# First norm by feature, gate columns behind the modulation stages, and split square sums in a hybrid recurrent layer

## The reference

```python
def rmsnorm(x, w):
    xf = x.astype(jnp.float32)
    y = xf * lax.rsqrt(jnp.mean(jnp.square(xf), axis=-1, keepdims=True) + EPS)
    return (y * w.astype(jnp.float32)).astype(x.dtype)
...
        mod = jax.nn.silu(c) @ w_ada[l] + b_ada[l]
        sh1, sc1, g1, sh2, sc2, g2 = [m[:, None, :] for m in jnp.split(mod, N_MOD, axis=-1)]
        h = rmsnorm(x, norm_mix[l]) * (1.0 + sc1) + sh1
...
    proj = h @ w_in
    hq, hf, hi, hog, gq, gk, gv, ga, gb, gz, gate_a, gate_b = split_cols(proj, IN_SIZES)
...
    o_hg = rmsnorm(o_hg, hg_norm) * jax.nn.silu(heads(hog, HG_DV).astype(jnp.float32))
...
    conv_out, s_conv_new = causal_conv(jnp.concatenate([gq, gk, gv], axis=-1), s_conv, conv_w)
```

## Time and profile before

| | |
|---|---|
| median of 3 runs | 949.81 us (949.46 to 950.88) |
| the profiled execution, its own time | 951.82 us |
| its span in the profile | 950.0 us |
| busy: PE | 923.8 us (97%) |
| busy: DVE | 669.4 us (70%) |
| busy: ACT | 438.2 us (46%) |
| busy: POOL | 105.6 us (11%) |

### The profile page before, as it was taken

The page is one execution under the profiler, slowest core; times in us unless marked ns, Lnnn a source line. Parts: engine busy times, 40 slices in busy tenths (PEclk is TensorE's granted clock), DMA queues, the critical chain, the costliest instruction groups (busy, mean ns, idle before and its releaser), DMA issues.

```text
span 950.0 us, 22427 instructions
## 1 busy us (share of the span) xinstructions
PE 923.8 (97%) x9425; PEld 892.8 (94%) x9425; DVE 669.4 (70%) x1254; ACT 438.2 (46%) x808; POOL 105.6 (11%) x133
## 2 busy tenths in 40 slices
PE   6999999999999999999999999999999999999997
PEld 6999888989999999999999999999999999999996
DVE  3778879866577677477766888889435899994553
ACT  6687445424223544553222257465322666662213
POOL 0110011112020110100100001122001222220000
PEclk9999999999999999999999999999999999999998
DMA  9834234444333432315643332232233343323222
GB/s 347 268 87 134 59 97 112 113 128 117 115 102 102 123 85 68 100 56 165 208 127 106 90 89 77 80 90 73 85 96 104 102 119 91 90 78 101 67 67 95
DMA packets 146175, 104.88 MB, mean 110 GB/s; under 512 B 5170, under 2 KB 139000, under 8 KB 144924
## 3 DMA queue, kind: packets, MB, share of 16 engines
q1 hardware_dynamic: 139099, 79.23, 28.6%
q0 software_dynamic: 6352, 22.00, 7.7%
q10 hardware_dynamic: 624, 2.23, 0.6%
HBM read 100.12 MB, written 3.31 MB: 109 GB/s over the span
## 4 chain that ended last, share of the span: by engine, by line
PE 48%; DVE 4%; ACT 3%; issue 2%; POOL 0%; DVEq 0%; ACTq 0%; POOLq 0%
PE G L2153 31%; PE G L2243 16%; DVE x_lo L1680 1%; DVE w_sum L1691 1%; DVE sum_lo L1700 1%; PE R L2164 0%; ACT w_hi L1306 0%; DVE w_lo L1700 0%; ACT w_hi L1219 0%; ACT b L1286 0%; ACT d_hi L1311 0%; POOL w_sum L1164 0%; PE R L2161 0%; DVE val L1711 0%; DVE w_lo L1592 0%
## 5 line engine op out<-in xcount | busy, mean ns | idle before, releaser
L2153 PE MATMUL G<-h_hi,w_hi 128*128 128x272 f32 (+1 forms) x880 | 263.7, 300 | 2.8 <-DVE ff_shift L2099 1.4
L2153 PE MATMUL G<-h_lo,w_hi 128*128 128x272 f32 (+1 forms) x880 | 253.8, 288 | 0.4 <-issue 0.4
L2153 PE MATMUL G<-h_hi,w_lo 128*128 128x272 f32 (+1 forms) x880 | 253.5, 288 | 0.1
L1592 DVE TENSOR_TENSOR w_lo<-raw,w_hi 128x1024 fp32r<-128x1024 f32 (+2 forms) x111 | 117.2, 1056 | 104.4 <-ACT w_hi L1219 103.6
L2153 PEld LDWEIGHTS G<-h_hi,w_hi 128*128 128x128 f32 x880 | 165.7, 188 | 6.2 <-DVE ff_shift L2099 1.7
L2153 PEld LDWEIGHTS G<-h_lo,w_hi 128*128 128x128 f32 x880 | 166.0, 189 | 0.6 <-issue 0.6
L2153 PEld LDWEIGHTS G<-h_hi,w_lo 128*128 128x128 f32 x880 | 165.7, 188 | 0.0
L1219 ACT ACTIVATE w_hi<-raw 128x1024 fp32r<-128x1024 f32 (+2 forms) x111 | 101.4, 914 | 90.6 <-PE G L2153 90.5
L1164 POOL TENSOR_TENSOR w_sum<-raw 128x512 f32<-128x512 f32 x36 | 50.1, 1395 | 318.3 <-DMA raw<-in_w_up 169.8
L2243 PE MATMUL G<-x_hi,sum_hi 128*128 128x272 f32 x288 | 83.7, 291 | 1.2 <-ACT partial L1322 1.1
L2243 PE MATMUL G<-x_hi,sum_lo 128*128 128x272 f32 x288 | 83.4, 290 | 0.0
(11 more groups left out here) (326 smaller groups left out, 2074.2 us busy)
## 6 DMA issues: line engine op xcount, KB each, us to landing
raw<-in_w_in SPq DMA_DIRECT2D x48, 512.0 KB, 4.1
raw<-in_w_up SPq DMA_DIRECT2D x44, 512.0 KB, 4.0
w_ada<-in_w_ada_t POOLq DMA_DIRECT2D x49, 256.0 KB, 3.2
wada<-in_w_ada_s SPq DMA_DIRECT2D x8, 1024.0 KB, 14.3
raw<-in_w_down SPq DMA_DIRECT2D x16, 320.0 KB, 3.2
raw<-in_w_out SPq DMA_DIRECT2D x8, 512.0 KB, 4.1
raw<-in_w_down SPq DMA_DIRECT2D x8, 512.0 KB, 4.1
w_ada_t<-in_w_ada_t POOLq DMA_DIRECT2D x15, 256.0 KB, 3.2
```

The lines of the kernel that those rows point to most:

```text
L1592: dve.tensor_tensor(lo, raw[:, i % RAW, 0:job.nk, 0:job.m], hi.bitcast(F32), ALU.subtract).then_inc(w_lo_done, 1)
L2153: ins = pe.matmul(out, w, x, start=(job.first and k == 0 and p == 0), stop=(job.last and k == job.nk - 1 and p == 2))
```

## The change

Three parts.

**First norm by feature.** x arrives by feature, in four DMAs of two tiles each (4352 bytes a partition) straight into xT. ACT squares eight tiles (128x544), DVE adds them up in acc (seven additions), PE sums acc over partitions with a matrix of ones (`in_sums`, fp32, 512 and 32 columns), ACT takes Ln twice and Exp, and has in_rn, 1/rms laid out over all partitions. DVE multiplies each xT tile by it (`in_norm`, eight, two ahead of each stage). x_diag, xtok and `x_first` are gone. The matrix of ones is set by POOL and no longer loaded. `c_cols` now stands behind `in_sums`.

**Order of the first jobs.** The two jobs in the stages are gk0 and gk1. gab comes behind: 36 of its 48 matmuls after the parts of stage 3 (`gab_part` 0), 12 after the duo (`gab_part` 1), in banks of R. gq0's weights get a place of their own ("third") and are split in stage 3. Within a stage, `duo_part` 2j-2 of both jobs stands ahead of `ada_rows` j. The evacuations come as gk0, gab, gk1. What stood inside gk1's job (g_sp, the split of job 4, g_a) stands inside gq0's, and each later group of extra steps is one job later too; the second pair's gk1 is taken out of the weave. The gate columns are loaded from a contiguous input. SP loads wada and raw weights in turn.

**Square sums of the heads' outputs.** In `o_sq` ACT squares twice (sq in fp32, sq_hi rounded) and DVE takes sq_lo = sq - sq_hi in place of the square; `onorm` is four rounded products for each head (hi and lo, 512 and 32 columns) in place of two fp32 ones.

```diff
-    for c in range(3):
-        do("x_sq", c)
-    do("x_first", 0)
-    do("x_sq", 3)
-    do("x_first", 1)
-    do("x_sq", 4)
     do("vectors")
-    do("x_first", 2)
+    for k in range(KD):
+        do("in_sq", k)
+    do("in_sums")
     do("c_cols")
-    do("x_first", 3)
-    do("x_first", 4)
+    do("in_norm", 0)
+    do("in_norm", 1)
     do("split", 0)
-    do("split", 1)
     do("ada_rows", 0)
     do("ada_T", 0)
     do("h1", 0)
     for j in range(1, STAGES):
+        do("in_norm", 2 * j)
+        do("in_norm", 2 * j + 1)
+        do("split", j)
+        do("duo_part", 2 * j - 2, 0)
+        do("duo_part", 2 * j - 2, 1)
         do("ada_rows", j)
-        do("duo_part", 2 * j - 2, 0)
+        do("duo_part", 2 * j - 1, 0)
         do("ada_T", j)
-        do("duo_part", 2 * j - 2, 1)
-        do("duo_part", 2 * j - 1, 0)
         do("duo_part", 2 * j - 1, 1)
         if j == STAGES - 1:
-            do("split_hi", 2)
+            do("gab_part", 0)
         do("h1", j)
-    do("split_lo", 2)
     do("sel")
...
-    duo(gagb, gk0)
-    around(gk1, [("g_sp",), ("split_hi", 4), ("g_a",), ("split_lo", 4)], [])
-    around(gq0, [("g_sq", 0, 2), ("g_scan",)], [])
...
+    evac = [s for s in plan[mark:] if s[0] == "evac"]
+    del plan[mark:]
+    plan.append(("duo", 0, 1))
+    do("gab_part", 1)
+    plan.extend([evac[0], evac[2], evac[1]])
+    around(gq0, [("g_sp",), ("split_hi", 4), ("g_a",), ("split_lo", 4)], [])
+    around(gq1, [("g_sq", 0, 2), ("g_scan",)], [])
...
-    weave(gdn_steps(0, ahead), parts_of(gk1, gq0, gq1, gv0, gv1, *hg_inputs("hf", 0), fine=True))
+    around(gk1, [("g_norm", 0, 1)], [])
...
+    weave(gdn_steps(0, ahead), parts_of(gq0, gq1, gv0, gv1, *hg_inputs("hf", 0), fine=True))
...
-                act.dma_start(xtok[:, c, :], t["x_prompt"][0, toks(c), :]).then_inc(x_in[c], 16)
...
+                act.dma_start(xT[:, 2 * j:2 * j + 2, :], t["x_t"][:, 2 * j:2 * j + 2, :]).then_inc(x_in[j], 16)
...
+                elif name == "in_sq":
...
+                    act.activation(sq[:, k % 2, :], xT[:, k, :], ACT.Square).then_inc(in_squared, 1)
...
+                elif name == "in_norm":
+                    k = a[0]
+                    dve.wait_ge(in_rn_ready, 1)
+                    dve.tensor_tensor(xT[:, k, :], xT[:, k, :], in_rn[:, :], ALU.mult).then_inc(in_normed, 1)
...
+            def sums_of_parts(n, hi, lo):
+                for j, cols_ in enumerate(GROUPS):
+                    fill(n, j, [mm(lambda b: R[:, b, 0:cols_.stop - cols_.start], ones[:, :], hi[:, cols_], True, False),
+                                mm(lambda b: R[:, b, 0:cols_.stop - cols_.start], ones[:, :], lo[:, cols_], False, True)])
```

More of the change, by code:

```diff
@@ L506, in make_plan @@
                 continue
-            while plan[at][0] not in ("job", "g_y", "g_u"):
+            while plan[at][0] not in ("half" if g == 1 else "job", "g_y", "g_u"):
                 at += 1
@@ L580, in build @@
     duos = [s[1:] for s in plan if s[0] == "duo"]
-    gab = duos[0][0]
-    aside = {gab: "rec", duos[1][1]: "ffn"}
+    gab_group = next(g for g, x in enumerate(groups) if x[0] == "gagb")
+    gab = groups[gab_group][2]
+    aside = {gab: "rec", gab + 1: "third", duos[1][1]: "ffn"}
     ending = len(groups) - 1
@@ L596, in build @@
     conv_no = {(arg[1], arg[3]): n for n, (_, arg, _) in enumerate(g for g in groups if g[0] == "conv")}
-    assert all(s[1] == i for i, s in enumerate(s for s in plan if s[0] == "evac"))
+    assert all(s[1] == i for i, s in enumerate(s for s in plan if s[0] == "evac") if i > gab_group)
     sq_no = {n: sum(x[0] in ("g_sq", "o_sq") for x in plan[:n]) for n in range(len(plan))}
@@ L798, in build @@
         const_in = sem("const_in")
+        ones_set = sem("ones_set")
+        squared = sem("squared")
         vec_in = sem("vec_in")
         ident_in = sem("ident_in")
-        x_in = [sem(f"x_in{c}") for c in range(CHUNKS)]
+        x_in = [sem(f"x_in{j}") for j in range(STAGES)]
         x_again = sem("x_again")
@@ L1069, in _ @@
                     sp.dma_start(wada01[:, j, v, :, :], t["w_ada_s"][j, v]).then_inc(ada_in[j], 16)
-            sp.dma_start(ones[:, :], t["all_ones"]).then_inc(const_in, 16)
+                if j <= gab:
+                    load(j)
             sp.dma_start(sel[:, :, :], t["head_select"]).then_inc(const_in, 16)
             sp.dma_start(masks_c[:, :, :], t["level_masks_c"]).then_inc(const_in, 16)
-            sp.wait_ge(fill_done, last_bank[spot("x_first", N_CHUNK)] + 1)
+            sp.wait_ge(fill_done, last_bank[spot("vectors")] + 1)
             sp.dma_start(masks_t[:, :, :], t["level_masks_t"]).then_inc(masks_in, 16)
             for n, step in enumerate(plan):
-                if step[0] == "job" or step[0] == "duo" and step[1]:
+                if step[0] == "job" or step[0] == "duo" and step[1:] != duos[0]:
                     for i in step[1:]:
@@ L1101, in _ @@
         def _(pool):
+            pool.memset(ones[:, :].bitcast(F32), 1.0).then_inc(ones_set, 1)
             for w in w_aside["rec"]:
@@ L1214, in split_weights @@
                     return
-                if i in aside:
+                if aside.get(i) == "ffn":
                     act.wait_ge(job_done, i - 2)
-                elif nth_ring[i] >= 2:
+                elif i not in aside and nth_ring[i] >= 2:
                     act.wait_ge(job_done, ring[nth_ring[i] - 2] + 1)
@@ L1391, in _ @@
                     link(act.activation(rows[:, 1, :], rows[:, 1, :], ACT.Exp))
-                    act.activation(rows[:, 1, :], rows[:, 1, :], ACT.Ln, bias=ones[0:NH, 0:1]).then_inc(sp_log, 1)
+                    act.activation(rows[:, 1, :], rows[:, 1, :], ACT.Ln, bias=ones[0:NH, 0:1].bitcast(F32)).then_inc(sp_log, 1)
                 elif name == "g_a":
@@ L1487, in _ @@
                     if kind == "gagb":
-                        wait_group(act, g)
-                        act.activation(halves(acc[0:QUAD + NH, :]), G[0:QUAD + NH, g % 2, :, 0:HALF], ACT.Copy)\
-                            .then_inc(slot_user["act"], 1)
+                        f = first_fill[spot("gab_part", 1)]
+                        for half in range(2):
+                            act.wait_ge(fill_done, f + half + 1)
+                            act.activation(halves(acc[0:QUAD + NH, :])[:, half, :], R[0:QUAD + NH, bank_of(f + half), 0:HALF],
+                                           ACT.Copy).then_inc(bank_user["act"], 1)
                     elif kind == "conv":
@@ L2286, in added @@
                             pe.wait_ge(acc_ready, 1)
-                            return pe.matmul(R[:, b, 0:cols_.stop - cols_.start], ones[:, :], acc[:, cols_],
+                            return pe.matmul(R[:, b, 0:cols_.stop - cols_.start], ones[:, :].bitcast(F32), acc[:, cols_],
                                              start=True, stop=True, skip_group_check=True)
@@ L2293, in _ @@
                     pe.wait_ge(acc_ready, 2 + turn)
-                    fill(n, 0, [mm(lambda b, c=c: R[0:length(c), b, 2 * c:2 * c + 2], x[:, toks(c)], ones[:, 0:2], x is acc, x is not acc)
+                    fill(n, 0, [mm(lambda b, c=c: R[0:length(c), b, 2 * c:2 * c + 2], x[:, toks(c)], ones[:, 0:2].bitcast(F32), x is acc, x is not acc)
                                 for c in chunks for x in (acc, sq[:, 0, :])])
```

204 lines of the change are left out of this document (121 added, 83 removed).

## The result

The changed kernel takes 988.62 us (median of 6 runs, 985.75 to 989.69) against 950.35 (6 runs, 949.46 to 953.18): slower by a factor of 1.0393 (1.0372 to 1.0414). The forecast was 967.0, with 958 to 975 as its range: the sign was right, the size less than half. The profiled execution took 988.09, its span is 986.2 against 950.0.

What follows compares the result with a forecast made beforehand. The prediction took PE, busy 923.8 of 950.0 us, to bound the kernel. Its terms, 17.9 - 2.1 + 0.7 + 0.8 = +17.3 us, gave 969.1 for the profiled execution and 967.0 for the median, range 958 to 975.

Steps and rivals of the forecast that it cites:

- T0: First modulation transpose in PE's timeline; forecast at 23.5 us, 1.7 later than before, with bounds of 19.3 to 24.5.
- my far bound of 13: Start of the kernel: the last x load was to land between 10.1 and 13 us, with 12.5 taken.
- the bad one: T0 with every bound on its bad side, put at 24.5 us.
- every bound on the good side: T0 with x landing at 10.1 us and PE at full pace, put at 19.3 us.
- From T0 to gq1: Stages and first jobs up to gq1's start: 48.8 us, so gq1 at 72.3, 17.9 later, 16.2 of it by waits.
- T1: Second modulation transpose in PE's timeline; forecast 10.4 us after T0.
- The weave: Recurrences with one filler job fewer among their small products: gain excluded, loss of up to 3 us, +0.7 taken.
- The clock: Some products run slow after 8.4 us of idle PE: +0.8 us taken, bounds 0 to 3.
- My rival for a thinned PE: Stages: PE stays at half pace there as the change thins its activity; 977 us in all, chance 0.08.
- The norms: Eight onorms, four rounded products each in place of fp32 ones: -2.1 us taken, bounds 0 to -5.0.
- My sign that PE's busy time would fall: Whole kernel: PE's busy time down by about 12 us for the transposing products and 2 for the norms.

## Why the prediction was right or wrong

**T0.** Forecast 23.5, measured 25.07. The last x landed at 13.4 us (ACT's last squares start at 13.36), just behind my far bound of 13 and not at 12.5. The sums began at 15.74, not 14.5, and ACT had them at 17.8, not at 16.3: late by 0.9 for x, 0.4 for the last squares and their addition, 0.3 for the sums. From there my steps held: SiLU at 21.0 (3.2 us on, as priced) and rows of 3.6 at half pace. The result is outside my own bounds: the bad one was 24.5 (and the terms with every bound on the good side add up to 18.7, not 19.3).

**From T0 to gq1.** Forecast 48.8 us, measured 49.3. The wait for h was 2.60 (2.9), the one for job 1's w_lo 2.04 (3.3; the products ahead of it took 1.4 at half pace instead of 0.75), T1 came 11.7 behind T0 (10.4), the next two stages took 7.2 each (7.0), with waits of 1.75 (1.95). The wait on gq1's w_lo was 7.14 (8.4). The chain of ACT and DVE that I had summed step by step is in the trace in that order, in 14.8 us (15.9), behind a duo that ended 34.5 after T0 (32.9). That the sum is right within 0.5 is partly luck: two errors nearly cancel.

**The weave: the step that failed.** "The weave has one filler job fewer among the small products of the recurrences: ... a loss of up to 3 (half a job) is not; I take +0.7." It was 17.0; with seven fillers back 15 us came back, and six fillers in the kernel before cost 16. Two errors are in that step. I took the loss for a matter of how much PE work there is, and looked at PE; it was DVE, with a split and four modulation sums piled up ahead of the copy into Tc, since the table that places the sums was not moved with the fillers. And I priced a wait at its own length, with no stretch at half pace behind it. For the first wait, moving three sums shows both (7 us less); the second (3.33 us, for S, with four more sums ahead of it on DVE, 183.05 to 185.87) was not tried, nor was the pause of 2.30 us, for which the view names no cause.

**The clock.** "... of that I take +0.8 (0 to 3)." At gq1 it was about 4.7 us at half pace, 2.1 lost, inside my bound. In the recurrence it was 20.5 us, about 9 lost: 7.4 measured in the first stretch, and an estimate of 1.7, half of its length, for the second. My rival for a thinned PE placed the half pace in the stages and gave it 0.08; the stages had it only from 28 to some 35 us. It happened where I had not looked, though the Trainium skill (TensorE: Matmul & The Clock Gate, What's actually happening) says in general that activity releases the throttle. The traces agree with that rule as far as it goes: 0.50 behind the waits of 2.21, 3.33 and 7.14 us, 1.00 where the last of these is filled with products, though pauses of 2.03 and 2.30 us had 1.00 behind them.

**The norms.** Forecast -2.1; -1.5 in the trace of the part alone, -1.0 in the changed kernel, near the small end of the bounds (0 to -5.0). My sign that PE's busy time would fall, by 12 for the transposing products and 2 for the norms, failed: it rose by 3.0, since the stretches at half pace count in it (7.4, 1.7 and 2.1 us above, among others).

Sum as forecast: 17.9 - 2.1 + 0.7 + 0.8 = 17.3. As traced: 20.0 to gq1's start, 1.6 more by the first norm, 17.0 in the recurrence, and the rest -2.4 (less than half of it the norms): 36.2.

## What to carry to other kernels

In a program whose order is written out, work that is moved out of a mix takes its neighbours' timing with it: see what the *other* engines have queued between two waits of the busy one, and move their small tasks along. A stall of the matrix engine is to be priced with the stretch at half clock that the trace may show behind it. Here that stretch was up to twelve times as long as the wait (17 us behind 1.42), and 17.1 us of it cost 7.4, so that a filler job is worth more than its own time. Where a late engine is a whole chain, reordering its steps moved the wait to the next customer; less work in the chain, or more cover, was not tried. And a gain at the end of a trace is to be followed back to where it arises: the 2.0 us of the filled wait came from elsewhere.

## What was not expected of the hardware

- A wait of 1.42 us (six fillers in the kernel before) was followed by some 17 us at a granted clock of 0.50, one of 2.21 (changed kernel) by 17.1, one of 3.33 by 3.4, and one of 7.14 by 4.7. In all four PE's busy time reads 100% or nearly so while the clock is down, so the busy share alone does not show the loss. The clock fell with a pause of 1.92 us too (sums moved), while waits of 1.75 in the later stages, one of 2.03 (seven fillers) and one of 2.30 (changed kernel, at 142) brought none. So the length of a wait alone decides neither whether the clock falls nor for how long; what does was not tried.
- In the first products of the kernel the records show half pace (0.21 us apiece; in the changed kernel 3.60 us for 64 products that take 1.95 later) while the granted clock reads 1.00 (0.99 in the changed kernel from 20 to 28 us). In the first 28 us the row of the clock does not show the pace.
- With 54 superfluous products PE did 7 us more work, and the program was not slower; nor was it faster for them.
- PE paused for 2.30 us at 142 in the changed kernel, and for 0.48 to 2.33 us near the same place in the runs that keep six fillers, with nothing in the view that released it. No run here tells what it was.
